# Delta branch: decays computed in the norm's block, head norms in the recurrence's block, a split setup of loads and credits

## The reference

```python
h = rms_norm_2(x, norm_g) @ w_in
gq, gk, gv, gb, ga, gg, dq, dk, dv, dg, mq, mg = split_cols(h, EV_SPLITS)
y = jnp.concatenate([
    gdn_branch(gq, gk, gv, gb, ga, gg, conv_w, a_log, dt_bias, gdn_gain),
    diff_attention(dq, dk, dv, dg, rel_table, dq_gain, dk_gain, lam, subln, lambda_init),
    memory_attention(mq, mg, mem, mem_norm, mem_w_kv, mem_qn, mem_kn),
], axis=-1)
return x + y @ w_out
```

## Time and profile before

| | |
|---|---|
| median of 3 runs | 2654.57 us (2654.33 to 2654.68) |
| the profiled execution | 2655.15 us |
| its span, first to last instruction | 2653.4 us |
| mean granted TensorE clock | 0.996 |
| PE busy | 2549.1 us (96%) |
| DVE, ACT, POOL busy | 1376.3, 887.2, 106.9 us |
| instructions | 37466 |
| HBM read | 520.76 MB, 199 GB/s over the span |

### The profile page before, as it was taken

One profiled execution on the slowest core, in us unless ns is written; L12 is line 12 of the kernel. 1 busy time (PEld: TensorE's weight loads), 2 busy tenths in 40 slices (PEclk: granted clock), 3 DMA queues, 4 the chain that ended last, 5 costly groups with the idle time before them and its releaser, 6 DMA issues. The chain is left out here.

```text
span 2653.4 us, 37466 instructions
## 1 busy us (share of the span) xinstructions
PE 2549.1 (96%) x13984; PEld 1691.1 (64%) x13984; DVE 1376.3 (52%) x2651; ACT 887.2 (33%) x1632; POOL 106.9 (4%) x116
## 2 busy tenths in 40 slices
PE   8999999999999999998998999999999999999999
PEld 7995455778554444445994775784555765674547
DVE  5654685566533333334774554555643545445435
ACT  5545211444311111113542431542323533441324
POOL 0001101011000000000000000000010000001000
PEclk9999999999999999999999999999999999999999
DMA  7754444455299999995442012554342552544234
GB/s 309 223 212 155 146 143 143 159 206 198 94 403 422 421 422 422 422 421 227 175 175 87 34 49 80 190 191 174 111 153 85 199 209 95 175 153 157 87 112 159
DMA packets 80593, 530.62 MB, mean 200 GB/s; under 512 B 9120, under 2 KB 13600, under 8 KB 19136
## 3 DMA queue, kind: packets, MB, share of 16 engines
q1 hardware_dynamic: 76416, 515.55, 51.4%
q0 software_dynamic: 3456, 11.02, 1.7%
q10 hardware_dynamic: 576, 2.10, 0.2%
HBM read 520.76 MB, written 7.86 MB: 199 GB/s over the span
## 5 line engine op out<-in xcount | busy, mean ns | idle before, releaser
L464 DVE TENSOR_TENSOR split_wl<-ring,split_wh 128x512 fp32r<-128x512 f32 x418 | 289.8, 700 | 207.9 <-ACT split_wh L430 204.5
L430 ACT ACTIVATE split_wh<-ring 128x512 fp32r<-128x512 f32 x418 | 262.6, 631 | 276.5 <-PE ps L400 272.4
L2300 PE MATMUL ps<-ring,yT 128*64 128x256 f32 x1984 | 237.0, 384 | 15.0 <-DMA ring<-in_weights 15.0
L779 PE MATMUL ps<-ring,xT 128*128 128x512 f32 x544 | 240.5, 594 | 8.8 <-PEq L3034 1.9
L537 PE MATMUL ps<-features_xh,features_wh 128*128 128x256 f32 x816 | 232.3, 285 | 1.2 <-DVE features_wl L518 1.2
L539 PE MATMUL ps<-features_xh,features_wl 128*128 128x256 f32 x816 | 230.8, 283 | 0.0
L398 PE MATMUL ps<-split_wh,split_xh 128*128 128x512 f32 x572 | 225.4, 394 | 0.0
L1155 PE MATMUL ps<-ring,xT 128*128 128x512 f32 x512 | 222.0, 592 | 2.8 <-PEq L554 1.7
L400 PE MATMUL ps<-split_wh,split_xl 128*128 128x512 f32 x572 | 222.6, 389 | 0.0
L399 PE MATMUL ps<-split_wl,split_xh 128*128 128x512 f32 x572 | 222.5, 389 | 0.0
L2300 PEld LDWEIGHTS ps<-ring,yT 128*64 128x64 f32 x1984 | 135.6, 136 | 112.6 <-issue 43.7
(11 more groups left out here) (657 smaller groups left out, 3982.6 us busy)
## 6 DMA issues: line engine op xcount, KB each, us to landing
ring<-in_weights SPq DMA_DIRECT2D x468, 1024.0 KB, 5.7
x_res<-in_x SPq DMA_DIRECT2D x1, 2048.0 KB, 7.5
yT<-in_mem SPq DMA_DIRECT2D x1, 2048.0 KB, 15.8
rel_skew<-lru_feat POOLq DMA_DIRECT2D x1, 2048.0 KB, 50.0
mem_features<-yT ACTq DMA_DIRECT2D x4, 512.0 KB, 7.3
s_wb<-in_s_bc POOLq DMA_DIRECT2D x4, 512.0 KB, 4.0
s_wc<-in_s_bc POOLq DMA_DIRECT2D x4, 512.0 KB, 4.0
gate_bias<-in_gate_bias POOLq DMA_DIRECT2D x8, 256.0 KB, 3.9
```

The lines of the kernel that those rows point to most:

```text
L430: nc.scalar.activation(wh[:, c % deep, :], raw(unit, turn, c), ACT.Copy).then_inc(w_high.sem, 1)
L464: last = nc.vector.tensor_tensor(wl[:, c % deep, :], raw(unit, turn, c), wh[:, c % deep, :], ALU.subtract)
L779: last = nc.tensor.matmul(k.ps[:, 2 * self.pairs[n] + t, :], x[:, kc, t * P:(t + 1) * P], k.ring[:, slot, c * BLK:(c + 1) * BLK], start=kc ...
L2300: last = nc.tensor.matmul(k.ps[s * WIN:(s + 1) * WIN, e, 0:FF], rows, k.ring[:, slot, at:at + FF], start=kc == 0, stop=kc == KC - 1)
```

## The change

`setup` loads x in two halves with an event each, and ident and cols on POOL's queue. The 124 credits are added by POOL (42), DVE (42) and ACT (40), none by PE. The ring's first loads are issued in the next block, and the waits for the loads stand at their first users. In `add_to_x` the wait for ACT's copy stands between the two adds. `rms_scale` waits for its row alone. The small product, the exponentials and the sigmoid of the decays are done in the even layer's norm block (`DecayInput`). The softplus runs on DVE in ten steps between the splits of the first column block of `gdn_in`, and the running sums on PE and DVE in the second block. The tail of `gdn_in` has six fill steps in place of the small product and `keep_busy`. The two head norm blocks are gone: q and k are normed at the head of `gdn_heads` on DVE, beside ten fill steps, and POOL clears the rooms there.

```diff
@@ add_to_x, finish_dve
         nc.vector.tensor_tensor(k.x[:, 1, ds(b * BLK, BLK)], k.ps[:, 2 * j + 1, :], k.x[:, 1, ds(b * BLK, BLK)], ALU.add)
+        wait_copied()
         return nc.vector.tensor_tensor(k.x[:, 0, ds(b * BLK, BLK)], copied[:, j % 2, :], k.x[:, 0, ds(b * BLK, BLK)], ALU.add)
@@ rms_scale
-                dve.wait_ge(k.loaded, k.loads)
+                dve.wait_ge(k.row_loaded, 16)
@@ norm_features
+                if early:
+                    act.wait_ge(k.x_loaded[t], 16)
...
+            if beside:
+                beside.activate(act)
...
+            if beside:
+                beside.product.prepare(dve)
...
             elif early:
+                arrived(pe)
+                pe.wait_ge(k.x_loaded[0], 16)
                 keep_busy(k, pe, 7, early, src[:, 0, :])
...
+            if beside:
+                fill.multiply(pe, 1)
+                pe.wait_ge(evac_a.sem, evac_a.at(groups // 2 - 1))
+                pe.wait_ge(evac_v.sem, evac_v.at(groups // 2 - 1))
+                beside.product.multiply(pe)
+                fill.multiply(pe, 1)
+                beside.product.add_up(pe)
+                fill.multiply(pe, after - 2)
...
         def _(sp):
+            if early:
+                stream(k, sp, RING)
@@ setup
-            sp.dma_start(k.x[:, :, :], k.dram["x"].rearrange("(t p) d -> p t d", p=P)).then_inc(k.first_loaded, 16)
-            sp.dma_start(k.ident[:, :], k.dram["ident"]).then_inc(k.first_loaded, 16)
-            sp.dma_start(k.cols[:, :], k.dram["cols"]).then_inc(k.first_loaded, 16)
+            for t in range(NT):
+                sp.dma_start(k.x[:, t, :], k.dram["x"][t * P:(t + 1) * P, :]).then_inc(k.x_loaded[t], 16)
             load(k, sp, k.rows[:, :], k.dram["rows"].to_broadcast([P, ROW_N]))
-            stream(k, sp, RING)
-            sp.wait_ge(k.first_loaded, 48)
...
-            for name in EVENTS[::2]:
-                pe.sem_inc(k.ev(name).sem, Event.CREDIT)
...
-            for name in EVENTS[1::2]:
+            pool.dma_start(k.ident[:, :], k.dram["ident"]).then_inc(k.first_loaded, 16)
+            pool.dma_start(k.cols[:, :], k.dram["cols"]).then_inc(k.first_loaded, 16)
+            for name in EVENTS[:third]:
                 pool.sem_inc(k.ev(name).sem, Event.CREDIT)
...
+            for name in EVENTS[third:2 * third]:
+                dve.sem_inc(k.ev(name).sem, Event.CREDIT)
...
+            for name in EVENTS[2 * third:]:
+                act.sem_inc(k.ev(name).sem, Event.CREDIT)
@@ gdn_in
+GDN_TAIL = (4, 2)
+    decay_after = {3 + n: n for n in range(DeltaDecay.STEPS)}
...
+                load(k, sp, masks[:, :, :, :], k.dram["gdn_masks"])
                 stream(k, sp, reach(base + blocks * upb))
                 sp.wait_ge(k.kv_stored, 32)
+                fill.load(sp, sum(GDN_TAIL))
...
+                        if b == 1 and kc == 7:
+                            pe.wait_ge(evac_a.sem, evac_a.at(0))
+                            pe.wait_ge(evac_v.sem, evac_v.at(0))
+                            delta.multiply(pe, masks)
+                        if b == 1 and kc == 11:
+                            delta.wait_taken(pe)
...
-                product.multiply(pe)
-                keep_busy(k, pe, 2, 8)
-                product.add_up(pe)
-                keep_busy(k, pe, 2, 22)
+                fill.multiply(pe, GDN_TAIL[0])
                 pe.wait_ge(evac_a.sem, evac_a.at(final))
                 pe.wait_ge(evac_v.sem, evac_v.at(final))
                 transpose(final, final, range(0, 2))
+                fill.multiply(pe, GDN_TAIL[1])
                 transpose(final, final + 1, range(2, 4))
...
+                            if b == 0 and kc in decay_after:
+                                delta.step(dve, decay_after[kc])
+                            if b == 1 and kc == 8:
+                                delta.take(dve)
@@ gdn_heads, PE
-            fill.multiply(pe, fill_steps)
+            fill.multiply(pe, 2)
+            for d in dirs:
+                sums(0, d)
+            fill.multiply(pe, fill_steps - 2)
+            for j in range(2):
+                wait(pe, "heads_normed", j)
+                turned(0, j)
+                gate_products(3)
+                grams(0, j)
             pe.wait_ge(fill_a.sem, fill_a.at(0))
             pe.wait_ge(fill_v.sem, fill_v.at(0))
-            gate_products(2)
-            delta.multiply(pe)
-            gate_products(2)
-            for d in dirs:
-                sums(0, d)
-            gate_products(1)
-            turns(0)
-            gate_products(1)
-            grams(0, 0)
-            grams(0, 1)
@@ gdn_heads, ACT
-            delta.exps(act)
+            delta.wait_cum(act)
+            differences(0)
+            nc.scalar.activation(k.stat[:, 0:2], k.ones[:, 0:2], ACT.Sqrt)
+            act.wait_ge(ms.sem, ms.at(0))
+            nc.scalar.activation(norm[:, 1, :], norm[:, 0, :], ACT.Sqrt).then_inc(root.sem, 1)
+            decay(0)
+            for d in dirs:
+                decay_beta(0, d)
+                copy(0, d)
             fill.store_act(act, fill_steps)
-            delta.wait_cum(act)
-            decays(0)
             delta.grow(act)
-            copies(0)
@@ gdn_heads, DVE
-            delta.begin(dve)
-            delta.first(dve)
+            square(1)
+            square(0)
+            nc.vector.tensor_scalar(norm[:, 0, :], norm[:, 0, :], 1.0, EPS, ALU.mult, ALU.add).then_inc(ms.sem, 1)
+            dve.wait_ge(root.sem, root.at(0))
+            nc.vector.reciprocal(norm[:, 0, :], norm[:, 1, :])
+            dve.drain()
+            nc.vector.tensor_scalar(factors(0), factors(0), float(P) ** -0.5, None, ALU.mult)
+            scale(1)
+            scale(0)
             fill.store_dve(dve, fill_steps)
-            delta.last(dve)
-            delta.take(dve)
+            wait(dve, "rooms_clear", 4)
             begin(0)
@@ gdn_heads, POOL
+            for r in side:
+                nc.gpsimd.tensor_copy(eye[r, :], k.ident[r, r]).then_inc(sig("rooms_clear"), 1)
+            for n in range(2):
+                nc.gpsimd.memset(XF_b[n][lo, :, hi], 0.0).then_inc(sig("rooms_clear"), 1)
+            nc.gpsimd.memset(XF_f[hi, :, lo], 0.0).then_inc(sig("rooms_clear"), 1)
```

More of the change, by code:

```diff
@@ L927, in to_features, with norm_features, arrived @@
     k.ended(tr=groups, evac_a=(groups + 1) // 2, evac_v=groups // 2)
-def norm_features(k, src, out, squares, dst, gain, fill=None, before=0, after=0, early=0):
+def norm_features(k, src, out, squares, dst, gain, fill=None, before=0, after=0, early=0, beside=None):
+    def arrived(eng):
+        if early:
+            eng.wait_ge(k.first_loaded, 32)
     nc, st = k.nc, k.stat
@@ L971, in _ @@
                 last.then_inc(evac_v.sem, 1)
+            if beside:
+                beside.take(dve)
             if fill:
@@ L1020, in setup @@
     k.loads = 0
+    third = -(-len(EVENTS) // 3)
     with nc.Block() as block:
@@ L1917, in moe @@
         by_token = k.sb(scope, "by_token", [P, NT, D])
+        ba_w = k.sb(scope, "gdn_ba_weights", [P, KC, 32])
         rms_scale(k, k.x, k.x, row=final, squares=by_token,
-                  ahead=lambda sp: load(k, sp, k.ba_w[:, :, :], k.dram["gdn_ba_w"]), fill=fill, steps=6)
-        norm_features(k, k.x, by_token, by_token, k.xT, "norm_ev", fill, 5, 5)
+                  ahead=lambda sp: load(k, sp, ba_w[:, :, :], k.dram["gdn_ba_w"]), fill=fill, steps=6)
+        beside = DecayInput(k, scope, ba_w)
+        norm_features(k, k.x, by_token, by_token, k.xT, "norm_ev", fill, 5, 5, beside=beside)
+        beside.product.end()
     fill.end()
@@ L3333, in _ @@
                 finish(final)
-                product.copy(act)
                 activate(final, final, slice(0, 2))
@@ L3338, in _ @@
                 copy_out(final, final + 1, 2, 2)
+                fill.store_act(act, sum(GDN_TAIL))
             @block.vector
@@ L3383, in _ @@
                         convolve(final, tap, some)
-                product.wait(dve)
-                nc.vector.tensor_copy(ba[:, :, :], product.all_sums())
-    k.used += blocks * upb
+                fill.store_dve(dve, sum(GDN_TAIL))
     steps = blocks * KC - LEAD
@@ L3391, in gdn_in, with __init__, activate, take @@
     k.ended(dve_a=blocks + 1, act_a=blocks + 1, pe_a=blocks + 1, act_b=blocks + 1)
-    product.end()
+    return fill
+class DecayInput:
+    def __init__(self, k, scope, w):
+        self.k, self.product = k, TiledProduct(k, scope, 32, 32, w, 0, 1)
+    def activate(self, act):
+        k = self.k
+        self.product.copy(act)
+        k.nc.scalar.activation(k.stat[:, 0:2], k.ones[:, 0:2], ACT.Exp)
+        k.delta.exps(act)
+    def take(self, dve):
+        self.product.wait(dve)
+        self.k.delta.begin(dve, self.product.all_sums())
 class DeltaDecay:
-    def __init__(self, k, scope, ba, masks):
-        self.k, self.ba, self.masks = k, ba, masks
+    def __init__(self, k, scope):
+        self.k = k
         self.cols = 2 * NT * GDN_HEADS
```

(3 more changed lines are left out.)

149 lines of the change are left out of this document (92 added, 57 removed).

## The result

The median went from 2654.45 us (4 runs, 2652.71 to 2654.68) to **2633.32 us** (4 runs, 2630.35 to 2633.47), a ratio of 0.9919 [0.9902, 0.9936]: 21 us less. The forecast was 2628.9, with 2625.5 to 2634.5 around it. Five more runs of the same program, on another chip, gave 2631.50 (2627.42 to 2632.59), ratio 0.9915 [0.9901, 0.9928]. The profiled execution took 2633.33, with a span of 2631.6 against 2653.4.

What follows compares the result with a forecast made beforehand. PE, busy 2549.1 of 2653.4 us, was taken as the bound. 2655.15 - 24.4 - 0.3 + 2.3 + 0.6 + 0.5 - 3.2 - 1.2 = 2629.45, less 0.58 (profile above median) gives 2628.9 us, range 2625.5 to 2634.5.

Steps and rivals of the forecast that it cites:

- The window: PE between the delta branch's input projection and the first inverse: 69.8 us becomes 45.4 (44.8 to 46.0), 24.4 saved.
- place (1): In the window, transposes of the last two tiles need a Silu ending at 10.7 us; PE arrives at 11.0, just covered.
- place (4): In the window, transposes of k wait for k's norm on DVE: at most 14.8 us against PE's 19.5, cover 4.7.
- The rival with POOL's lock: Norm late because POOL clears rooms while DVE squares, blocking shared ports: 7.3 us over the cover, 2638.2 us; chance 0.04.
- First inverse: The first inverse starts at full clock and finds the second direction begun: 0.3 us less (0 to 0.8).
- The small product: Its 32 records and four summing records move into the norm's block, where PE finishes last: +2.3 us.
- Log sums: The log sums move into the projection's second column block: +0.6 us.
- softplus: Ten DVE steps between first-block splits and the taking of sums into the second: +0.5 us for both blocks (0 to 6).
- PE runs up to four splits behind DVE: Step in the first two column blocks: DVE's lead supports taking only +0.5 us for its added work.
- The rival of full exposure: DVE paces the first two column blocks, all softplus steps and sums exposed: +5.5 us more, 2634.4; chance 0.13.
- The start: Setup block ends at about 6.1 us, transposes start at about 12.8 instead of 16.03: 3.2 us less (1.5 to 4.2).
- The ends of two projections: First last-block add on DVE runs beside ACT's copy: 2 x 0.6 = 1.2 us less (0 to 1.4).

Runs made afterwards that it cites:

- experiment 5: Changed kernel with eight fill steps instead of four ahead of the last transposes, four instead of eight behind the sums: median 2631.78 us.
- experiment 4: Changed kernel with the two log sums on PE behind split 5 of the second column block instead of split 7: median 2630.13 us.

## Why the prediction was right, and where it was off

- **The window, -24.4 predicted, -25.4 measured.** Every step of the order stood where it was put, and PE waited for nothing but the restart (0.94). The 1.0 is in the size of a group: I took a step at 1.76, its busy time with the tail, and from start to start it is 1.72 (32 records, 13.73 us); transposes and grams likewise (0.44 and 0.89 to 0.99 where I took 0.52 and 1.05). 22 steps alone are 0.9 less. The lower bound of 44.8 was not low enough.
- **Its covers.** The thinnest is place (1): the last Silu ended at 1400.72 and PE's transposes start at 1400.77, with the two steps ahead of them 0.05 us longer than in experiment 5, so this cover is used up. k's norm came at 1416.6 and PE at 1421.32, the 4.7 us of place (4), and experiment 5 found its edge. The rival with POOL's lock fell: its five operations took 2.3 us in all, and DVE lost 0.5. The Trainium skill's page SBUF — State Buffer, section Who interferes with whom, has a DVE operation with two SBUF inputs contend with a GpSimd operation that reads SBUF; the square beside POOL's copy, 1.29 against 1.23, is at most a trace of that; the 0.43 behind it, ahead of a sum with one input, went too when POOL had nothing to do.
- **First inverse, -0.3 predicted, -0.32 measured.** The low clock after 1450 us, shown by the earlier trace rows, is gone.
- **The small product, +2.3 predicted, +2.51 measured**, the same within 0.03 in each profile of the changed kernel.
- **Log sums +0.6 and softplus +0.5 predicted, +1.91 measured.** The sums are 0.64. The 0.5 for DVE was too small, 1.27 (the mend of experiment 4 gives it back), and its reason was wrong: not DVE's load but its wait for PE's sums cost, since it spent the lead of the splits. The step that failed is "PE runs up to four splits behind DVE": behind a DVE that waits for PE there is no such lead. Adding the wait's line to DVE's queue, as the sum had not done, would have shown it. The rival of full exposure, 5.5 more, fell, but its sign, PE waiting for DVE's splits, was there twice, and the 1.91 came close to the 2 us at which the prediction called itself wrong.
- **The start, -3.2 predicted, -1.2 measured**, outside the 1.5 to 4.2 of the prediction. This is the main error. The step that failed is "With the table load behind them the block ends at about 6.1". The credits ran as I took them or faster (ACT's table load at 3.51, the last engine's at 5.0), but POOL's end of block was set by the landing of its own transfers, a wait that the sum didn't have. Its transposes came at 14.81 instead of the predicted 12.8; with the two loads on SP they came at 12.86. By the rule that the prediction cites from the Trainium skill (page DMA: Bandwidth & Descriptors, section SWDGE vs HWDGE vs iDMA: the two kinds of queue served in turn) ident should land early, beside x. Issued behind both halves of x it landed at 6.9, between the first at 5.6 and the second at 9.1, which agrees. On SP's queue it landed at 5.8, so the rule had no part in the miss.
- **The ends of two projections, -1.2 predicted, -1.3 measured**, at both places.
- **The granted clock, not predicted.** The sum had the clock only inside the window. Two falls in the profile of after, each of 1.6 us, and a smaller one at the end of the expert stage (3.4 us of missing clock against 5.1, over stretches of 1 us) make +3.3 and about -1. Where they come is a matter of the execution. With the start (+2.0), the projection (+0.8), the product (+0.2), the window (-1.0) and the recurrence (-0.4) they make +3.9 of the 4.4 us between 2628.9 and 2633.3; the rest is the 0.58 that the prediction took off because its profile lay above its median, which the new one does not. Without the two falls it would be 2630.0; the one run of 2630.35 may be of that kind, but it has no profile.
- **How much of it was luck.** 2633.3 lies 0.4 below the upper bound that the prediction had from its own terms, 2633.7. The start and the two falls, which the sum didn't have, came to 5.3 us against it; that the number is still inside is owed to the window's 1.0, to the smaller fall behind the expert stage and to a range with room for other terms. The main term, the window, was right by its mechanism.
- What stays open: 0.4 us of the way to the first expert product and 0.35 of the last thousand us are not assigned, nor the 0.36 by which the recurrence got shorter, and why the clock falls behind a wait of 0.7 us in one execution and not in another was not tried.

## What to carry to other kernels

Look at what an engine's end of block waits for: here POOL, with two transfers on its queue, was not free until they had landed (3.93 us), and SP, with three on its way, was (0.12). Put such loads on a queue whose drain doesn't wait, or leave nothing of the block behind them. When work is slipped between the steps of an engine that runs ahead of PE, look at its waits first: a wait for PE's own product costs the lead, and moving that product two steps forward cost nothing here. When single executions differ by as much as the edit is worth, compare stretches between fixed milestones of the traces, and not medians: here the window repeats within 0.02 us and the projection within 0.04, while stretches in which the clock may fall, or in which DMA works at full share, vary by one to two.

## What was not expected of the hardware

- POOL's drain lasted 3.93 us, to the landing of the two transfers that it had issued; SP's took 0.12 with three on their way, and POOL's without transfers 0.04.
- The clock went to its 1.2 GHz level behind waits of 0.48 and 0.73 us a few records apart (1586 us) in six of thirteen profiles, behind 2.18 us of idle time (726 us) in four, and behind 1.91 us (289 us) in seven; each fall cost 1.6 to 1.7 us.
- Of the 5.3 us that PE waits between the expert stage and the next block, with the DMA engines at full share, 2.6 could be filled with matmuls without moving the block. Behind dummies of 8.79 and of 2.75 us PE waited 2.56 and 2.83 more, and in both the clock fell among the first products behind this wait.
